# A fused block's mixture-of-experts end: 192 slots per expert, and token sums made by an accumulating DMA

## The reference, cut to what matters

```python
def grouped_moe(x, router_w, router_bias, w_gate, w_up, w_down):
    scores = jax.nn.sigmoid(xt @ router_w)                 # 1024 tokens x 16 experts
    sel = scores + router_bias
    ...                                                    # the best group of 4 experts, its best 2
    gate = gate / gate.sum(-1, keepdims=True)
    ...                                                    # rows sorted by expert, in blocks
    def expert_block(args):
        hb = jax.nn.silu(xb @ w_gate[ei]) * (xb @ w_up[ei])
        return hb @ w_down[ei]
    ...
    y = (yb[dest].reshape(T, TOP_K, D) * gate[..., None]).sum(1)

ff = grouped_moe(x, router_w, router_bias, w_gate[l], w_up[l], w_down[l])
x = layer_norm(DEEPNORM_ALPHA * x + ff, ln_moe_g[l], ln_moe_b[l])   # alpha = 2 ** 0.25, eps = 1e-5
```

## Time and profile before

| | |
|---|---|
| median of 3 runs | 3250.75 us (3249.36 to 3257.69) |
| profiled execution | 3254.93 us, of which the span is 3253.5 us |
| PE busy | 2872.8 us, 88% of the span |
| DVE, ACT, POOL busy | 1018.4, 638.9, 112.2 us |
| mean granted TensorE clock | 0.942 of full |
| start of the first expert gather to the end of the last down product | 2786.8 to 3174.2 us |
| from there to the end of the span | 79.3 us |

### The profile page before, as it was taken

One profiled execution on the slowest core, in us unless ns is written; L12 is line 12 of the kernel. 1 busy time (PEld: TensorE's weight loads), 2 busy tenths in 40 slices (PEclk: granted clock), 3 DMA queues, 4 the chain that ended last, 5 costly groups with the idle time before them and its releaser, 6 DMA issues.

```text
span 3253.5 us, 31047 instructions
## 1 busy us (share of the span) xinstructions
PE 2872.8 (88%) x12358; PEld 1900.8 (58%) x12358; DVE 1018.4 (31%) x2566; ACT 638.9 (20%) x1627; POOL 112.2 (3%) x140
## 2 busy tenths in 40 slices
PE   6799999997899999999998988768899898799990
PEld 3478767643577666777643655533454655577760
DVE  3334404513022222222424354434400334211116
ACT  2234313301122222222311111100000200011112
POOL 1000000000000000000000000000000000100003
PEclk9899999898999999999999988888899999799995
DMA  3000010311110111001132000003230122366635
GB/s 129 26 1 1 8 58 1 102 68 46 26 27 1 27 27 27 1 7 46 39 111 68 26 4 26 26 0 123 102 111 0 52 99 86 119 222 222 231 130 213
DMA packets 149109, 214.81 MB, mean 66 GB/s; under 512 B 18144, under 2 KB 103008, under 8 KB 148960
## 3 DMA queue, kind: packets, MB, share of 16 engines
q1 hardware_dynamic: 142048, 187.59, 17.6%
q0 software_dynamic: 6912, 25.17, 2.4%
HBM read 174.86 MB, written 37.75 MB: 65 GB/s over the span
## 4 chain that ended last, share of the span: by engine, by line
PE 81%; DVE 10%; ACT 3%; issue 2%; DMA 1%; POOL 0%; DVEq 0%; ACTq 0%; SPq 0%; POOLq 0%
PE banks L167 75%; PE banks L170 6%; ACT arena L1211 1%; POOL arena L2290 0%; DVE arena L2404 0%; DVE arena L1816 0%; DVE arena L1489 0%; DVE arena L963 0%; DVE arena L1791 0%; DVE arena L967 0%; DVE arena L2581 0%; ACT arena L928 0%; DVE arena L2595 0%; DVE arena L2593 0%; DVE arena L700 0%
## 5 line engine op out<-in xcount | busy, mean ns | idle before, releaser
L167 PE MATMUL banks<-arena 128*128 128x256 f32 (+8 forms) x10166 | 2669.1, 420 | 127.4 <-DVE arena L1800 26.2
L167 PEld LDWEIGHTS banks<-arena 128*128 128x128 f32 (+2 forms) x10166 | 1669.2, 196 | 990.4 <-issue 763.6
L170 PE MATMUL banks<-arena 128*128 128x128 f32 (+1 forms) x2000 | 328.0, 290 | 174.0 <-DVE arena L1713 28.3
L170 PEld LDWEIGHTS banks<-arena 128*128 128x128 f32 (+1 forms) x2000 | 252.9, 150 | 262.7 <-issue 108.3
L634 ACT ACTIVATE arena<-banks,arena 128x128 f32<-128x128 f32 (+3 forms) x192 | 142.1, 740 | 335.3 <-DVE arena L659 334.3
L659 DVE TENSOR_REDUCE arena<-banks 128x1 f32<-128x128 f32 (+3 forms) x192 | 145.5, 758 | 154.0 <-PE banks L167 152.1
L671 DVE COPY arena<-banks 128x512 f32<-128x512 f32 (+2 forms) x144 | 75.9, 527 | 274.6 <-PE banks L170 274.4
L249 POOL TENSOR_TENSOR arena<-arena 128x1 f32<-128x1 f32 (+1 forms) x88 | 66.1, 752 | 2729.9 <-DVE arena L1083 1620.0
L680 DVE SCALAR_TENSOR_TENSOR arena<-banks,arena 128x64 f32<-128x64 f32 x192 | 54.4, 283 | 230.3 <-PE banks L167 229.1
L700 DVE SCALAR_TENSOR_TENSOR arena<-arena,banks 128x128 f32<-128x128 f32 x128 | 36.0, 281 | 190.4 <-ACT arena L696 190.4
L1211 ACT ACTIVATE arena<-banks 64x512 f32<-64x512 f32 x64 | 37.9, 592 | 209.2 <-PE banks L167 198.3
(11 more groups left out here) (246 smaller groups left out, 1186.1 us busy)
## 6 DMA issues: line engine op xcount, KB each, us to landing
arena<-in_o_w_in_dram SPq DMA_DIRECT2D x32, 512.0 KB, 6.9
x_scratch<-arena SPq DMA_DIRECT2D x32, 512.0 KB, 2.8
arena<-x_scratch SPq DMA_DIRECT2D x32, 512.0 KB, 4.2
arena<-in_w_gate_dram SPq DMA_DIRECT2D x16, 1024.0 KB, 8.8
arena<-in_w_up_dram SPq DMA_DIRECT2D x16, 1024.0 KB, 10.8
arena<-in_w_down_dram SPq DMA_DIRECT2D x16, 1024.0 KB, 6.2
slot_out<-arena SPq DMA_DIRECT2D x32, 512.0 KB, 3.1
arena<-in_x_dram SPq DMA_DIRECT2D x16, 512.0 KB, 4.6
```

The lines of the kernel that those rows point to most:

```text
L167: return pe.matmul(o, a, b, start=start, stop=stop)
L170: return pe.transpose(o, a, ident)
```

## The change

1. `LIMIT` becomes 192 and an expert has 192 slots, in a block of 128 and one of 64 (`WIDTHS`). Gate and up have 192 columns instead of 256; the second block's gather, transposes, copies and down product have 64 rows.
2. `out4` stores each normed tile twice, to `x4` and to a new tensor `x5` (1024 rows and 128 more). `x5` is where the sums are made.
3. `dve_route` makes a second table `PUT` beside `IDX` (the token of each slot, for an empty slot one of the 128 extra rows), and the gates are divided by alpha. A new pair `pe_slot_gates` and `dve_slot_gates` makes `GSL`, the gate of each slot, by 16 DVE products and 16 small matmuls behind gate and up of expert 0.
4. ACT and DVE scale the down results by `GSL` as they take them out of the banks.
5. `slot_out` and its stores are gone. POOL issues for each block an indirect DMA that adds `YS` to `x5` (a "put"). Each put waits until the one before it has landed. In POOL's order the two gathers of expert e+2 stand ahead of the two puts of expert e.
6. SP loads down of expert e+1 when down of expert e-1 is done.
7. The end loads eight tiles of `x5`, and has statistics, norm, gain and bias alone; the norm's epsilon is divided by alpha squared. Gain and bias are loaded at the start of the expert stage.

```diff
-LIMIT = 256
+LIMIT = 192
+WIDTHS = (128, 64)
+NS = 192
...
-            vec.tensor_scalar(IDX[:, :], bank(6)[:, 0:32], float(S - 1), None, MIN).then_inc(r_index.sem, 1)
+            vec.tensor_scalar(IDX[:, :], bank(6)[:, 0:32], float(S), float(S - 1), ADD, MIN).then_inc(r_index.sem, 1)
+            vs(vec.tensor_scalar(GSL, bank(6)[:, 0:32], 0.0, CST[:, C_TI:C_TI + 1], ALU.is_ge, MUL))
+            vs.done()
+            vec.scalar_tensor_tensor(PUT[:, :], bank(6)[:, 0:32], float(S), GSL, ADD, ADD).then_inc(r_index.sem, 1)
...
+        def dve_slot_gates():
+            for j in range(16):
+                vec.tensor_scalar(ROW[:, 128 * j:128 * j + 128], IO, LO[:, j:j + 1], G12[:, j:j + 1], ALU.is_equal,
+                                  MUL).then_inc(r_grow.sem, 1)
+            V.wait_ge(r_gs, 1)
+            vec.tensor_copy(GSL, bank(6)[:, 0:32]).then_inc(gs_done.sem, 1)
...
-            for j in range(32):
-                G.wait_ge(xg_turned, 2 * (j - 3))
-                rows(XG[j % 4], x4, IDX[:, j:j + 1], d_xg[j % 4])
+            gather(0)
+            gather(1)
+            for e in range(16):
+                if e + 2 < 16:
+                    gather(e + 2)
+                for b in range(2):
+                    j, w = 2 * e + b, WIDTHS[b]
+                    G.wait_ge(ys_a, j + 1)
+                    G.wait_ge(ys_v, j + 1)
+                    G.wait_ge(d_put, 16 * j)
+                    pool.indirect_dma_start(out=x5, out_offset=bass.IndirectOffsetOnAxis(
+                        ap=PUT[0:w, j:j + 1].bitcast(U32), axis=0), in_=YS[j % 3][0:w, :], in_offset=None,
+                        compute_op=ADD).then_inc(d_put.sem, 16)
...
+            for e in range(1, 16):
+                Y.wait_ge(gu_done, e)
+                if e + 3 < 16:
+                    load_expert(e + 3)
+                if e + 1 < 16 and e >= 1:
+                    Y.wait_ge(dn_done, 2 * e)
+                    load_down(e + 1)
...
+                if e == 0:
+                    pe_slot_gates()
...
-                V.wait_ge(d_yb[t], 16)
-                V.wait_ge(yc_done, t + 1)
-                vs(vec.scalar_tensor_tensor(ya, OTf[t], G2[:, t:t + 1], ya, MUL, ADD))
-                vs.done()
-                vs(vec.scalar_tensor_tensor(buf, buf, ALPHA, ya, MUL, ADD))
-                vs.done()
-                dve_layer_stats(s, buf)
+                V.wait_ge(d_fin[t], 16)
+                dve_layer_stats(s, OTf[t], LN_EPS / ALPHA ** 2)
```

More of the change, by code:

```diff
@@ L1819, in dve_layer_stats, with dve_out_ln @@
             vs.done()
-            vec.tensor_scalar(s[:, 14:15], s[:, 13:14], LN_EPS, None, ADD).then_inc(eps_done.sem, 1)
-        def dve_out_ln(st, before, xb, gains, stored):
+            vec.tensor_scalar(s[:, 14:15], s[:, 13:14], eps, None, ADD).then_inc(eps_done.sem, 1)
+        def dve_out_ln(st, before, xb, gains, stored, per=16):
             meet(V, before)
@@ L2072, in program @@
         x_out4 = x_block()
-        s_out4 = [d.block(16 * 4) for d in d_sn]
+        s_out4 = [d.block(32 * 4) for d in d_sn]
         x4_stored = over(*d_sn)
@@ L2107, in sp_out4 @@
             load_down(1)
[L2108 removed]
+            sp_out_ln(out4, x3, x4, x5)
             Y.wait_ge(proj_done, out4.proj + NT)
@@ L2295, in pool_moe @@
                 G.wait_ge(d, n)
-            G.wait_ge(r_index, 1)
             meet(G, out4_over)
-            G.wait_ge(route_over, 1)
-            for j in range(32):
-                G.wait_ge(xg_turned, 2 * (j - 3))
-                rows(XG[j % 4], x4, IDX[:, j:j + 1], d_xg[j % 4])
[L2302 to L2307, removed]
+            G.wait_ge(r_index, 2)
@@ L2309, in sp_moe @@
         def sp_moe():
+            meet(Y, out4_over)
             for d, n in x4_stored:
                 Y.wait_ge(d, n)
[L2312 to L2326, removed]
+            load(XB[0], row(ln_moe_g_2[0]), d_g)
@@ L2328, in pe_moe_turn @@
+            load(XB[1], row(ln_moe_b_2[0]), d_g)
+            for e in range(1, 16):
[5 more added lines that the diff above has]
+                    load_down(e + 1)
         def pe_moe_turn(e):
             for b in range(2):
-                j = 2 * e + b
+                j, w = 2 * e + b, WIDTHS[b]
                 P.wait_ge(d_xg[j % 4], 16 * (j // 4 + 1))
@@ L2333, in pe_moe_turn @@
                 P.wait_ge(xt_v, j)
-                turn_tile(XG[j % 4], xg_turned)
+                for half in range(2):
+                    for k in range(4):
+                        c = 512 * half + 128 * k
+                        m = pe.transpose(bank(4 + half)[:, w * k:w * k + w], XG[j % 4][0:w, c:c + 128], ident[0:w, 0:w])
+                    m.then_inc(xg_turned.sem, 1)
         def pe_moe():
@@ L2440, in program @@
         HS = [scr(40 + 2 * i, 512) for i in range(2)]
-        HF = [scr(44 + i, 256) for i in range(2)]
+        HF = [scr(44 + 2 * i, 256) for i in range(2)]
         def sp_all():
-            for d, n in ys_stored:
-                Y.wait_ge(d, n)
-            Y.wait_ge(d_ya, 16 * FIRST)
+            Y.wait_ge(d_put, 512)
+            Y.wait_ge(xg_turned, 64)
+            Y.wait_ge(gu_done, 16)
+            Y.wait_ge(dn_done, 32)
+            load(OT, x4.rearrange("(t p) c -> p t c", p=128), fb_x4)
             for e in range(16):
@@ L2523, in all_end, with sp_last @@
             eng.wait_ge(fb_st, 16 * NT)
-        yc_done, fin_shift, last_norm = event("first_row_scaled"), event("mean_scaled"), event("last_normed")
+        mean_scaled, last_norm, last_gain = event("mean_scaled"), event("last_normed"), event("last_gained")
         fin = Step(False)
-        s_fin = [d.block(16 * 4) for d in d_sn]
-        moe_over = [(ys_a, 32), (ys_v, 32), (dn_done, 32), (gu_done, 16), (xg_turned, 64)]
-        def pool_last():
-            meet(G, ys_stored)
-            meet(G, moe_over)
-            for t in range(NT):
-                rows(OTf[t], slot_out, DI[:, 8 + t:9 + t], d_yb[t])
-                if t + FIRST < NT:
-                    rows(YA[t + FIRST], slot_out, DI[:, t + FIRST:t + FIRST + 1], d_yl[t])
+        d_fin = [event(f"sum_landed_{t}") for t in range(NT)]
+        d_out = event("output_stored")
+        def sp_last():
+            Y.wait_ge(d_put, 512)
+            Y.wait_ge(xg_turned, 64)
+            Y.wait_ge(gu_done, 16)
+            for t in range(NT):
+                load(OTf[t], x5[128 * t:128 * t + 128, :], d_fin[t])
+            for t in range(NT):
+                Y.wait_ge(xn_done, fin.xn + t + 1)
+                sync.dma_start(out[0][128 * t:128 * t + 128, :], OTf[t]).then_inc(d_out.sem, 16)
+            Y.wait_ge(d_out, 16 * NT)
+        def pool_last():
             for t in range(NT):
```

182 lines of the change are left out of this document (77 added, 105 removed).

## The result

Five runs of the changed kernel gave a median of 3276.45 us (3270.13 to 3281.03), against 3250.89 us (3249.36 to 3257.69) before: ratio 1.0076, 95% interval 1.0058 to 1.0094. The profiled execution took 3280.94 us with a span of 3279.6.

A forecast was written before the change was run, and what follows sets the result against it. PE bounds the old kernel; after the change a circle through POOL sets the pass at 22.1 us. Passes 28.7, start -2.5 and end 23.0 sum to 49 us gained, on the median 3202 us, range 3165 to 3308.

## What to carry to other kernels

When a DMA that waits for results is put on a queue that also prefetches, draw the circle from the result back to itself through that queue, and add every link, wake-ups and the clock after PE's wait included; if the sum is near the engine's own pass, move the prefetch ahead of the waiting one. Here the prefetch's buffers had been free a whole pass earlier, so the cure cost nothing and was worth 100 us, in a loop where the waits between puts still fit beside PE's 20.2 us. A gain in the engine that was the bound (52 us by 192 slots) is only seen once such a circle is open.

## What was not expected of the hardware

- An indirect DMA that adds 128 rows of 4 KB to HBM landed in 6.2 us, against 3.4 for one that writes them, and held POOL for 1.60 us against 0.99 (64 rows: 1.44 against 0.91).
- Sixty-five matmuls of idle work in PE's waits shortened the kernel by 32 us.
- POOL started a DMA 0.7 to 0.8 us after the copy or the landing that it waited for, put and plain write alike.
- Alternating between 128-wide and 64-wide stationary tiles costs PE 0.14 to 0.19 us at each change (3.58 and 3.63 us a block of down, 3.43 to 3.44 where both are 128 wide).
